# Eight RMS norms between the dense stages: pair sums, a full-matrix mean, ln and exp, and the next stage's low parts moved into their VectorE loop

## What is computed

```python
def rms_norm(x, g, eps=RMS_EPS):
    xf = x.astype(jnp.float32)
    y = xf * lax.rsqrt(jnp.mean(xf * xf, axis=-1, keepdims=True) + eps)
    return (y * g.astype(jnp.float32)).astype(x.dtype)
```

## Time and profile before

| | |
|---|---|
| median of three runs | 4151.31 us (4148.47 to 4154.32) |
| the profiled execution | 4149.06 us |
| its span (first to last instruction) | 4147.3 us |
| PE busy | 3558.6 us (86%) |
| VectorE busy | 2091.7 us (50%) |
| ScalarE busy | 1239.5 us (30%) |
| mean granted clock of TensorE | 0.924 of full speed |

### The profile page before, as it was taken

How to read it: one execution, slowest core, us unless ns; L and a number is a source line. 1 busy time by engine, 2 the same in 40 slices (tenths; PEclk the granted TensorE clock), 3 DMA queues, 4 the chain that set the end, 5 groups by cost and what they waited for, 6 DMA issues and landing times. The chain is left out here.

```text
span 4147.3 us, 57357 instructions
## 1 busy us (share of the span) xinstructions
PE 3558.6 (86%) x23427; PEld 2930.3 (71%) x23427; DVE 2091.7 (50%) x2898; ACT 1239.5 (30%) x1632; POOL 0.2 (0%) x4
## 2 busy tenths in 40 slices
PE   7789999997999897699988799966358757979998
PEld 5567888776788786588866688856257645768886
DVE  3475745436655545553454543444655457335334
ACT  2253423324433313322233322222311123223222
POOL 0000000000000000000000000000000000000000
PEclk9899999997999998799989899978579978989998
DMA  3101222220222221122221122212000010122221
GB/s 132 65 0 57 95 92 100 92 102 1 91 101 92 93 81 51 41 81 101 91 81 71 51 97 96 95 52 71 0 8 4 7 37 1 51 71 92 92 101 61
DMA packets 43842, 280.12 MB, mean 68 GB/s; under 512 B 5967, under 2 KB 7119, under 8 KB 11156
## 3 DMA queue, kind: packets, MB, share of 16 engines
q1 hardware_dynamic: 36576, 266.35, 18.0%
q10 hardware_dynamic: 7092, 11.21, 0.8%
HBM read 275.44 MB, written 2.11 MB: 67 GB/s over the span
## 5 line engine op out<-in xcount | busy, mean ns | idle before, releaser
L164 DVE TENSOR_TENSOR WL<-W,WH 128x2048 fp32r<-128x2048 f32 x254 | 582.1, 2292 | 881.6 <-ACT WH L154 876.0
L231 PE MATMUL PS<-XH,WH 128*128 128x512 f32 x2288 | 894.8, 391 | 3.8 <-issue 2.3
L233 PE MATMUL PS<-XH,WL 128*128 128x512 f32 x2288 | 890.4, 389 | 0.0
L232 PE MATMUL PS<-XL,WH 128*128 128x512 f32 x2288 | 890.3, 389 | 0.0
L154 ACT ACTIVATE WH<-W 128x2048 fp32r<-128x2048 f32 x254 | 485.6, 1912 | 1209.4 <-PE PS L321 678.9
L231 PEld LDWEIGHTS PS<-XH,WH 128*128 128x128 f32 x2288 | 429.5, 188 | 99.5 <-issue 10.9
L232 PEld LDWEIGHTS PS<-XL,WH 128*128 128x128 f32 x2288 | 429.5, 188 | 90.8 <-issue 2.2
L233 PEld LDWEIGHTS PS<-XH,WL 128*128 128x128 f32 x2288 | 429.5, 188 | 89.5
L319 PE MATMUL PS<-HH,WH 128*128 128x512 f32 (+1 forms) x1024 | 401.6, 392 | 10.5 <-DVEq L95 9.3
L320 PE MATMUL PS<-HL,WH 128*128 128x512 f32 (+1 forms) x1024 | 399.9, 391 | 0.0
L321 PE MATMUL PS<-HH,WL 128*128 128x512 f32 (+1 forms) x1024 | 399.8, 390 | 0.0
(11 more groups left out here) (442 smaller groups left out, 4359.8 us busy)
## 6 DMA issues: line engine op xcount, KB each, us to landing
W<-in_weights SPq DMA_DIRECT2D x254, 1024.0 KB, 4.7
X<-in_x ACTq DMA_DIRECT2D x1, 2048.0 KB
out<-X ACTq DMA_DIRECT2D x1, 2048.0 KB, 7.1
bias<-bias_spread ACTq DMA_DIRECT2D x4, 256.0 KB
wide_consts<-in_consts ACTq DMA_DIRECT2D x1, 642.0 KB
w_gd<-in_w_gd ACTq DMA_DIRECT2D x1, 640.0 KB
rope<-in_c_rope ACTq DMA_DIRECT2D x1, 528.0 KB
ws<-in_ws ACTq DMA_DIRECT2D x1, 512.0 KB
```

The lines of the kernel that those rows point to most:

```text
L164: P.e.tensor_tensor(K.WL[:, s, :], K.W[:, s, :], K.WH[:, s, :].bitcast(F32), ALU.subtract).then_inc(P.sem("weights_split"), P.adds("weight ...
L231: P.e.matmul(out, wh[:, k, c], xh[:, k, r], start=(k == 0), stop=False)
L232: P.e.matmul(out, wh[:, k, c], xl[:, k, r], start=False, stop=False)
L233: last = P.e.matmul(out, wl[:, k, c], xh[:, k, r], start=False, stop=(k == KT - 1))
```

## The change

- The eight slices of squares are summed in pairs, three adds that don't depend on each other (slices 2 and 3, 4 and 5, 6 and 7) in place of six in two chains.
- PE multiplies slices 0, 1, 2, 4 and 6 by the full 128x128 matrix of 1/1024, five accumulating fp32 products of 128x512 (twice 128x264 in N6 and N7), so the mean stands on all partitions at once. The first two need squares only, not the adds.
- ScalarE reads the mean from PSUM and takes ln(mean + epsilon), then exp(-0.5 times that), 128x512 each, into `K.R` in SBUF. The table set with both is loaded ahead, behind `split_last`. The steps of lines 683, 687, 694 and 663 are gone.
- VectorE multiplies by `K.R`. Each product is added to X one slice behind, not two, and, in N1 to N4, the low part of the `from_raw` stage that follows (`raw_low`, the old line 466) is made two slices behind in the same loop. ScalarE makes the high parts of that stage as before.

```diff
@@ -397,6 +397,14 @@
...
+def raw_low(K, P, raw, k):
+
+    src, gain = raw
+    P.e.wait_ge(P.sem("norm_hi"), P.due("norm_hi"))
+    P.e.scalar_tensor_tensor(K.XL[:, k, 0:S], src[:, k, 0:S], gain[:, k:k + 1], K.XH[:, k, 0:S].bitcast(F32),
+                             ALU.mult, ALU.subtract).then_inc(P.sem("norm_lo"), P.adds("norm_lo"))
+
+
@@ -423,7 +431,7 @@
...
     after_norm = after_narrow = after_sums = False
-    scaled = False
+    scaled = low_done = False
     raw = None
@@ -440,6 +448,8 @@
 
     def pe(self, K, P):
         wide_pe(K, P, self.n, self.xh, self.xl, self.toks, self.after_norm, self.after_narrow, self.raw is not None)
+        if self.raw is not None:
+            P.count("norm_squared", KT)
 
     def act(self, K, P):
         start_loads(K, P, self.early_loads)
@@ -460,11 +470,9 @@
 
     def dve(self, K, P):
         if self.raw is not None:
-            src, gain = self.raw
-            for k in range(KT):
-                P.e.wait_ge(P.sem("norm_hi"), P.due("norm_hi"))
-                P.e.scalar_tensor_tensor(K.XL[:, k, 0:S], src[:, k, 0:S], gain[:, k:k + 1], K.XH[:, k, 0:S].bitcast(F32),
-                                         ALU.mult, ALU.subtract).then_inc(P.sem("norm_lo"), P.adds("norm_lo"))
+            if not self.low_done:
+                for k in range(KT):
+                    raw_low(K, P, self.raw, k)
             split_last(K, P, split_dve)
             P.e.wait_ge(P.sem("norm_squared"), P.due("norm_squared", KT))
             for half in (4, 2, 1):
@@ -621,15 +629,13 @@
     before_norm = False
     after_sums = before_panels = False
 
-    def blocks(self):
-
-        out = [(part, c, min(128, tn - c)) for part, (t0, tn) in enumerate(self.toks) for c in range(0, tn, 128)]
-        return sorted(out, key=lambda b: -b[2])
-
-    def columns(self, K):
-
-        n, rows = len(self.blocks()), self.blocks()[-1][2]
-        return [K.R[:, 0:4]] + ([K.R[0:rows, 4:n]] if n > 4 else [])
+    next_raw = None
+
+    def mean(self, K):
+
+        if len(self.toks) == 2:
+            return both_parts(K, 0), parts(K.R[:, 0:self.t1 - self.t0])
+        return K.PS[:, 0, 0:self.toks[0][1]], K.R[:, 0:self.toks[0][1]]
 
     def act(self, K, P):
         start_loads(K, P, self.early_loads)
@@ -638,11 +644,12 @@
                 P.e.wait_ge(P.sem("sum_stored"), P.due("sum_stored"))
             P.e.activation(K.Y[:, k, self.t0:self.t1], self.src[:, k, self.t0:self.t1], ACT.Square).then_inc(P.sem("norm_squared"), P.adds("norm_squared"))
         split_last(K, P, split_act)
-        P.e.wait_ge(P.sem("norm_inverse"), P.due("norm_inverse"))
-        for r in self.columns(K):
-            last = P.e.activation(r, r, ACT.Sqrt)
-        last.then_inc(P.sem("norm_root"), P.adds("norm_root"))
-        P.count("norm_mean", 1)
+        P.e.preload_act_table_set("natural_log_exp_and_others")
+        mean, r = self.mean(K)
+        P.e.wait_ge(P.sem("norm_mean"), P.due("norm_mean"))
+        P.e.activation(r, mean, ACT.Ln, bias=K.eps_col[:, 0:1]).then_inc(P.sem("act_order"), P.adds("act_order"))
+        P.e.wait_ge(P.sem("act_order"), P.due("act_order", 0))
+        P.e.activation(r, r, ACT.Exp, scale=-0.5).then_inc(P.sem("norm_root"), P.adds("norm_root"))
         if self.out is None:
             for k in range(KT):
                 P.e.wait_ge(P.sem("norm_scaled"), P.due("norm_scaled"))
@@ -651,17 +658,17 @@
 
     def pe(self, K, P):
 
-        P.e.wait_ge(P.sem("norm_summed"), P.due("norm_summed"))
-        for j, (part, c, n) in enumerate(self.blocks()):
-            t = self.toks[part][0] + c
-            for half in range(2):
-                last = P.e.matmul(K.PS[0:n, 0, 2 * j:2 * j + 2], K.Y[:, half, t:t + n], K.inv_d[:, 0:2], start=(half == 0), stop=(half == 1))
+        for k in (0, 1, 2, 4, 6):
+            if k < 2:
+                P.e.wait_ge(P.sem("norm_squared"), P.due("norm_squared"))
+            else:
+                P.e.wait_ge(P.sem("norm_partial"), P.due("norm_partial"))
+            if k == 0 and len(self.toks) == 2:
+                P.e.wait_ge(P.sem("norm_squared"), P.due("norm_squared", 0, less=-1))
+            for part, (t0, tn) in enumerate(self.toks):
+                last = P.e.matmul(K.PS[:, part, 0:tn], K.inv_d[:, :], K.Y[:, k, t0:t0 + tn], start=(k == 0), stop=(k == 6))
         last.then_inc(P.sem("norm_mean"), P.adds("norm_mean"))
-
-        for j, (part, c, n) in enumerate(self.blocks()):
-            P.e.wait_ge(P.sem("norm_diagonal"), P.due("norm_diagonal"))
-            last = P.e.matmul(K.PS[:, 6 + part, c:c + n], K.ones_row[0:n, 0:128], K.R[0:n, 16 + 128 * (j % 4):16 + 128 * (j % 4) + n], start=True, stop=True)
-            last.then_inc(P.sem("norm_spread"), P.adds("norm_spread"))
+        P.count("norm_squared", KT - 2)
         if self.out is None and not self.before_panels:
             P.count("norm_lo", KT)
         if self.gives_sums:
@@ -669,57 +676,37 @@
 
     def dve(self, K, P):
 
-        for k in range(2, KT):
-            P.e.wait_ge(P.sem("norm_squared"), P.due("norm_squared", 3 if k == 2 else 1))
-            if k >= 4:
-                P.e.wait_ge(P.sem("norm_partial"), P.due("norm_partial", 0, less=1))
-            y = K.Y[:, k % 2, self.t0:self.t1]
-            last = P.e.tensor_tensor(y, y, K.Y[:, k, self.t0:self.t1], ALU.add)
-            last.then_inc(P.sem("norm_summed" if k == KT - 1 else "norm_partial"), P.adds("norm_summed" if k == KT - 1 else "norm_partial"))
+        for k in (2, 4, 6):
+            P.e.wait_ge(P.sem("norm_squared"), P.due("norm_squared", 4 if k == 2 else 2))
+            y = K.Y[:, k, self.t0:self.t1]
+            P.e.tensor_tensor(y, y, K.Y[:, k + 1, self.t0:self.t1], ALU.add).then_inc(P.sem("norm_partial"), P.adds("norm_partial"))
         split_last(K, P, split_dve)
-        blocks = self.blocks()
-        P.e.wait_ge(P.sem("norm_mean"), P.due("norm_mean"))
-        for j, (part, c, n) in enumerate(blocks):
-            last = P.e.tensor_scalar(K.R[0:n, j:j + 1], K.PS[0:n, 0, 2 * j:2 * j + 1], self.eps, None, ALU.add)
-        last.then_inc(P.sem("dve_order"), P.adds("dve_order"))
-        P.e.wait_ge(P.sem("dve_order"), P.due("dve_order", 0))
-        for r in self.columns(K):
-            last = P.e.reciprocal(r, r)
-        last.then_inc(P.sem("norm_inverse"), P.adds("norm_inverse"))
+        P.count("norm_mean", 1)
         P.e.wait_ge(P.sem("norm_root"), P.due("norm_root"))
-        for j, (part, c, n) in enumerate(blocks):
-            if j >= 4:
-                P.e.wait_ge(P.sem("norm_spread"), P.due("norm_spread"))
-            at = 16 + 128 * (j % 4)
-            P.e.tensor_scalar(K.R[0:n, at:at + n], K.ident[0:n, 0:n], K.R[0:n, j:j + 1], None, ALU.mult).then_inc(P.sem("norm_diagonal"), P.adds("norm_diagonal"))
-        P.e.wait_ge(P.sem("norm_spread"), P.due("norm_spread", min(4, len(blocks))))
-        two = len(self.toks) == 2
-        r = K.PS[:, 6:8, 0:self.toks[0][1]] if two else K.PS[:, 6, 0:self.toks[0][1]]
-        view = (lambda ap: ap.rearrange("p (a n) -> p a n", a=2)) if two else (lambda ap: ap)
-        lag = 2
-        for k in range(KT + lag):
+        r = K.R[:, 0:self.t1 - self.t0]
+        for k in range(KT + 2):
             if k < KT:
-                src = view(self.src[:, k, self.t0:self.t1])
+                src = self.src[:, k, self.t0:self.t1]
                 g = self.gain[:, k:k + 1]
-                y = view(K.Y[:, k, self.t0:self.t1])
+                y = K.Y[:, k, self.t0:self.t1]
                 if self.out is None:
                     P.e.scalar_tensor_tensor(y, src, g, r, ALU.mult, ALU.mult).then_inc(P.sem("norm_scaled"), P.adds("norm_scaled"))
                 elif self.add:
                     P.e.scalar_tensor_tensor(y, src, g, r, ALU.mult, ALU.mult).then_inc(P.sem("norm_term"), P.adds("norm_term"))
                 else:
-                    last = P.e.scalar_tensor_tensor(view(self.out[:, k, 0:self.t1 - self.t0]), src, g, r, ALU.mult, ALU.mult)
+                    last = P.e.scalar_tensor_tensor(self.out[:, k, 0:self.t1 - self.t0], src, g, r, ALU.mult, ALU.mult)
                     if self.before_raw:
                         last.then_inc(P.sem("sum_stored"), P.adds("sum_stored"))
-            if k >= lag:
-                y = K.Y[:, k - lag, self.t0:self.t1]
-                if self.out is None:
-                    P.e.wait_ge(P.sem("norm_hi"), P.due("norm_hi"))
-                    P.e.tensor_tensor(self.xl[:, k - lag, self.t0:self.t1], y,
-                                      self.xh[:, k - lag, self.t0:self.t1].bitcast(F32), ALU.subtract).then_inc(P.sem("norm_lo"), P.adds("norm_lo"))
-                elif self.add:
-                    P.e.wait_ge(P.sem("norm_term"), P.due("norm_term", 0, less=min(lag, KT - 1 - (k - lag))))
-                    o = self.out[:, k - lag, self.out_off + self.t0:self.out_off + self.t1]
-                    P.e.tensor_tensor(o, o, y, ALU.add).then_inc(P.sem("sum_stored"), P.adds("sum_stored"))
```

(13 more changed lines are left out.)

## The result

| | before | changed |
|---|---|---|
| median of four runs | 4149.89 us (4148.36 to 4154.32) | 4116.40 us (4113.19 to 4119.57) |
| profiled execution | 4149.06 us | 4118.24 us |
| its span | 4147.3 us | 4116.5 us |
| mean granted clock | 0.924 | 0.933 |

The account below looks back on a forecast made before the run. PE runs without gaps in dense stages, so time is to be had where it stands still, at the eight norms. Their gains sum to 36.9 us: 4149.06 to 4112.2, and 4114.5 for the median; range 4103 to 4132.

Parts of the forecast that it names:

- The chain: Adds to first product of a norm: 6.1 us instead of 10.73, 4.6 us earlier in each of the first five.
- rival of cold products: Rival: the norms' products run at half clock, six chains losing up to 4.3 us each; some 26 us, 4140; 12%.
- Table load: Load for ln and exp: 1.28 us, covered by PE's products; by the skill's 2.66 us, 1 us lost in all.
- N6 and N7: Sixth and seventh norms: products begin at half clock; first product 3.4 us (1.8 to 4.3) and 4.2 us (2.4 to 5.0) earlier.
- N8: Last norm: first multiply at 4129.25 instead of 4134.19, 4.9 us earlier, 4.0 if the last product is cold.
- N3 and N4: Third and fourth norms: openings wait for the seventh sum, losing 2.1 and 1.6 us; net gains 2.5 and 3.0.
- panel count: Panels before the first four norms: 102, 118, 151, 163; at odd parity the opening waits for the seventh stored sum.
- N2: Second norm: opening starts at +3.9 us, PE later waits 2.6, 1.6 charged for the clock; gain 6.6 (4.8 to 8.3).
- N1: First norm: with low parts in the loop and a 13.0 us opening, it ends 3.1 us earlier; 7.7 in all.
- N2's paced opening: Rival: the second norm's opening, paced by VectorE, stays at half clock; 5 us less than in the sum, 4119.5; 8%.
- slower rival: Rival: the clock stays at half through products and openings; 56 us lost against 37 won, 4169; 4%.

Follow-up runs that it names:

- late_products: The changed kernel with all five products waiting for the last pair sum; 4144.60 us, ratio to before 0.9988.
- first_sum: The changed kernel with the opening behind a norm waiting for the first of eight stored sums, whatever the banks; 4104.80 us, ratio to before 0.9894.
- after: The changed kernel itself, as in the result, against the kernel before; median 4116.40 us, ratio 0.992.
- after_again: The repeat: the changed kernel run again with no edit; 4111.31 us, ratio to before 0.9908.
- root_inverse: The changed kernel with root (ScalarE) and inverse (VectorE) of 128x512 in place of ln and exp; 4137.53 us, ratio to before 0.9973.

## Why the prediction was right

**Direction and size.** Forecast 4114.5, range 4103 to 4132; measured 4116.4, and 4111.3 in the repeat. The sum of 36.9 us stands against 37.7 in the eight norms; the stretches between took 6.9 back in the first profiled execution and 0.4 in that of the repeat, so these 6.9 are spread, in the main, and not a term of the change. That the median came within 2 us of the forecast is luck: the repeat of the same kernel lies 5 us lower.

**The chain**, 4.6 us predicted and 4.85 measured, five times over. Five products of 0.86 us at full clock with their tail: 4.56 us. The other 0.25 us is mostly PE's start, 0.1 us ahead of the adds where I had put 0.2 behind. The products started after a pause of 0.83 us and ran at full clock. The rival of cold products was real: 2 us more of waiting brought it about in four of five chains (late_products). I had argued it away with the length of the pause, which was the right argument, but gave no number for how near the edge is.

**Table load.** It is not on the path: ln waits for PE 0.93 us longer than the load in N2. N8 has the least room:

```profile
4099.86 1.28 ACT L647 ACT_TABLE_LOAD   x1
4101.79 0.69 ACT L650 ACTIVATE R<-PS,wide_consts 128x512 f32<-128x512 f32 x1 [0.64 <-PE PS L669]
```

The Trainium skill's 2.66 us for a switch with its drain (ScalarE: Activation LUTs, What ACT_TABLE_LOAD costs) does not show here: ln follows PE's last product 1.93 us after the start of the load.

**N6 and N7**, 3.4 and 4.2 predicted, 3.43 and 3.71 measured: partly cold products of 7.5 and 7.6 us, where I had taken 7. That N6 fits to 0.03 us is luck: in the executions with the same chain it gained between 3.4 and 4.8 us, by where the clock rose. **N8** 4.9 and 4.90.

**N3 and N4**, 2.5 and 3.0 predicted, 2.3 and 3.0 measured. Two small errors offset each other: the chains gave 0.25 us more, and from first multiply to mean 2.6 and 1.8 us were lost where I had 2.1 and 1.6. The terms of the panel count add up to 106 as written; the total of 102 is right (4896 dense matmuls run before N1's first multiply, 48 a panel), the 4 in front of the 12 does not belong there, and the parity is the same either way. Counting panels to find the parity was the step that mattered: a wait that never showed in the trace of before, since it was always over, was what the change ran into; first_sum shows it by removing it.

**N2** is the term that was mis-sized, 6.6 against 8.4, by two errors. The opening was to start at +3.9 us; it started at +5.46, since at even parity it waits for the third sum, which the text of the kernel says and my step left out. It cost nothing, as the sum of squares ends at +20.2 us in any case, which I had. And I charged 1.6 us for a fall of the clock behind PE's pause. The pause was 1.7 us, not 2.6: the opening started later and PE's last matmul of it ended at +18.55, not at +17.6. In the four executions of the new norm in which this opening starts at +5.46 or +5.47 (after, after_again, late_products and root_inverse, with pauses of 1.5 to 1.9 us) the stretch behind it did not grow: 351.6 us each time, 351.5 before. With pauses of 2.24, 2.58 and 2.26 us in first_sum it did in the last two, by 1.8 and 1.7 us. So such a pause can have that price, and here it had none. **N1** came out 0.7 us short: its opening took 13.8 us where I had put 13.0; the granted clock came back 5.9 us after the opening's start. In the repeat it came back after 3.0 us, the opening took 12.4, and N1 gave 8.4 us.

**N2's paced opening** was no paced stream. It began at half clock, where PE needs 2.6 us a slice, and from its first matmul on low parts were always ready: PE has no gap in it. From 1750.45 to 1757.96 it runs at full clock with 0.68 us for three matmuls, 1.37 us a slice against VectorE's 1.92, and the windows from 1758 to 1762 show 1.00. So the fear of this rival, PE kept at half clock by VectorE's pace, was not put to the test here. The nearest to it are N3 and N4 of first_sum: two pauses of 0.27 us each between slices, PE busy for 10.46 of the 11 us from 2120 to 2131, and the granted clock at 1.00. The Trainium skill's rule on streams with frequent small pauses (TensorE: Matmul & The Clock Gate, A second HAM failure mode: psum-queue depth-cycling) would have cost 5 us here by the prediction's working; no opening shows the clock fall again after its return, but with so few pauses that says little about the rule.

**The slower rival** needed the openings to stay at half clock, and none did.

## What to carry to other kernels

When work is moved ahead of something that used to come first, list every wait of the engine that profits, those too that no trace shows because they were always over, and work out the value each waits for; here a wait by bank number took two of four gains away. Where two engines feed each other through a chain, let the matrix engine's share start early: with 2 us more of waiting the same new chain gained between 2.7 us and nothing instead of 4.9, partly by the wait itself and partly by the clock. And when a gain comes out smaller than its parts, look for the next thing on the path (here a sum of squares that used to be hidden): with both waits out of the way the same move was worth four times as much.

## What the runs showed that I had not expected

- A stretch of some 580 us whose code no version touches took between 577.7 and 586.1 us in nine profiled executions with the new chain, with TensorE's clock falling in other places each time; with the old chain it took 579.8 and 577.2 in two. Whether the new chain itself adds something there can't be told from these. Differences of 3 to 6 us between two versions of this kernel need several runs on one chip.
- Pauses of 1.5 to 1.9 us of PE in front of the mean left the clock alone in all four places. Of three pauses of 2.2 to 2.6 us, two cost 1.7 and 1.8 us. Behind the pauses of 2.97 to 2.98 us in late_products the five products took 4.53 us in N1 and 5.93 to 7.48 us in N2 to N5. So between 2.2 and 3.0 us the length of the pause alone does not say whether the clock falls.
- An inverse of 128x512 on VectorE costs 3.35 us, more than ln and exp of that tile on ScalarE with both hand-overs (1.38 us from ln's start to the first multiply).
